# A conditioning product moved from the first expert stage's norms to behind the fourth feed-forward, with another order of work at the norm after the second cross attention

## What is computed

```python
# first block, second layer's end (x: 256 x 1024)
#   x = layer_norm(ALPHA * x + memory_cross_attention(x, mem, wq, wkv, wo), g, b)
#   x = layer_norm(ALPHA * x + ..., ...)   with swiglu_ffn: (silu(g) * u) @ w_out
# second block
for layer in range(DEPTH):                    # DEPTH = 2
    mod_l = split(silu(c)     @ ada_w[layer] + ada_b[layer], 6)
    mod_c = split(silu(c_ctx) @ ada_w[layer] + ada_b[layer], 6)
    h_l = rms_norm(lat, norm1_w[layer]) * (1.0 + mod_l[1]) + mod_l[0]
    h_c = rms_norm(cx,  norm1_w[layer]) * (1.0 + mod_c[1]) + mod_c[0]
    y_l, y_c = hyena_mixer(...) if layer == 0 else swa_mixer(...)
    lat = lat + mod_l[2] * y_l
    h_l = rms_norm(lat, norm2_w[layer]) * (1.0 + mod_l[4]) + mod_l[3]
    lat = lat + mod_l[5] * expert_choice_ffn(h_l, router[layer], w_gate[layer], w_up[layer], w_down[layer])
    # the same for cx in layer 0
return rms_norm(lat, final_norm_w)
```

## Time and profile before

| | us |
|---|---|
| median of 3 runs | 2714.54 |
| lowest, highest | 2710.27, 2716.71 |
| span of the profiled execution | 2712.6 |
| PE busy, share of the span | 2477.5, 91% |
| DVE busy | 1459.2, 54% |
| ACT busy | 503.5, 19% |
| POOL busy | 124.4, 5% |
| DMA moved | 712.30 MB, mean 263 GB/s |

### The profile page before, as it was taken

How to read it: one execution, slowest core, us unless ns; L and a number is a source line. 1 busy time by engine, 2 the same in 40 slices (tenths; PEclk the granted TensorE clock), 3 DMA queues, 4 the chain that set the end, 5 groups by cost and what they waited for, 6 DMA issues and landing times. The chain is left out here.

```text
span 2712.6 us, 37104 instructions
## 1 busy us (share of the span) xinstructions
PE 2477.5 (91%) x14598; PEld 1707.6 (63%) x14598; DVE 1459.2 (54%) x2343; ACT 503.5 (19%) x945; POOL 124.4 (5%) x134
## 2 busy tenths in 40 slices
PE   8999999999999979999999799999998987777786
PEld 8997768999999668997676333333334773333233
DVE  7768536776876558767888722232234552112113
ACT  0004414100100231003331111111110541111111
POOL 1000000000000001003221100000000000000000
PEclk9999999999999999999999999999999998888989
DMA  7668542656456456552224899999996329999997
GB/s 239 245 224 293 184 163 81 207 186 201 164 186 217 151 201 228 186 188 78 62 62 163 310 421 422 422 422 422 422 422 270 125 95 409 422 422 422 422 422 322
DMA packets 234434, 712.30 MB, mean 263 GB/s; under 512 B 12677, under 2 KB 134549, under 8 KB 178912
## 3 DMA queue, kind: packets, MB, share of 16 engines
q1 hardware_dynamic: 223328, 675.85, 64.8%
q0 software_dynamic: 9856, 32.16, 3.6%
q10 hardware_dynamic: 1152, 2.93, 0.3%
HBM read 708.69 MB, written 2.20 MB: 262 GB/s over the span
## 5 line engine op out<-in xcount | busy, mean ns | idle before, releaser
L863 PE MATMUL work<-ring,scratch 128*64 128x512 f32 (+1 forms) x3008 | 552.4, 636 | 112.7 <-DMA ring<-in_moe_up 74.2
L863 PE MATMUL work<-rows_h_parts,ring_parts 128*128 128x256 f32 x3072 | 549.7, 285 | 11.2 <-ACT rows_h_parts L1769 6.6
L863 PEld LDWEIGHTS work<-rows_h_parts,ring_parts 128*128 128x128 f32 x3072 | 477.0, 194 | 14.9 <-issue 9.8
L863 PEld LDWEIGHTS work<-ring,scratch 128*64 128x64 f32 (+1 forms) x3008 | 144.6, 126 | 496.2 <-issue 278.7
L863 PE MATMUL work<-cols_x_parts,ring_parts 128*128 128x256 f32 x1536 | 414.9, 286 | 0.0
L2207 DVE TENSOR_TENSOR ring_parts<-ring,ring_parts 128x2048 fp32r<-128x2048 f32 x132 | 302.6, 2292 | 4.5
L863 PEld LDWEIGHTS work<-cols_x_parts,ring_parts 128*128 128x128 f32 x1536 | 287.8, 195 | 1.5
L863 PE MATMUL acc<-ring_parts,rows_h_parts 128*128 128x512 f32 x960 | 279.8, 391 | 0.0
L2822 DVE COPY scratch<-work 128x512 f32<-128x512 f32 x32 | 22.1, 692 | 373.4 <-PE work L863 373.4
L863 PE MATMUL work<-scratch 128*128 128x256 f32 (+4 forms) x1040 | 197.2, 377 | 6.5 <-issue 4.2
L863 PEld LDWEIGHTS acc<-ring_parts,rows_h_parts 128*128 128x128 f32 x960 | 177.0, 188 | 35.8 <-issue 1.0
(11 more groups left out here) (314 smaller groups left out, 2893.2 us busy)
## 6 DMA issues: line engine op xcount, KB each, us to landing
ring<-in_moe_down SPq DMA_DIRECT2D x128, 1024.0 KB, 25.9
ring<-in_moe_up SPq DMA_DIRECT2D x127, 1024.0 KB, 26.6
ring<-in_moe_gate SPq DMA_DIRECT2D x121, 1024.0 KB, 25.4
ring<-in_ffn_w_in SPq DMA_DIRECT2D x88, 1024.0 KB, 7.5
ring<-in_ada_w SPq DMA_DIRECT2D x48, 1024.0 KB, 9.7
ring<-in_ffn_w_out SPq DMA_DIRECT2D x44, 1024.0 KB, 6.8
ring<-in_xa_wkv SPq DMA_DIRECT2D x16, 1024.0 KB, 6.9
ring<-in_da_w_qkv SPq DMA_DIRECT2D x12, 1024.0 KB, 7.0
```

The costliest lines, as they stand in the source:

```text
L863: ins = nc.tensor.matmul(o, lhsT, rhs, start=start, stop=stop, **kw)
```

## The change

The product `ada(3)`, with its 8 loads on SP, its copy on ACT and its `store_mods(3)` on POOL, goes from the middle of `moe_norm0` to right behind `ffn(3)`. At `xa_norm1` three orders change: PE makes `xa_out1` half by half (both token tiles' first 512 columns, then the second), with DVE's waits in `layer_norm` numbered to match; ACT copies all of the context's tiles before the two roots of `xa_norm1`, and does both roots before `ada_out(2)`; DVE splits `ffn(3)`'s first weights behind the norm (in `ffn`) instead of ahead of it. `xa_out0`, `da_out` and `sw_out` keep their order. In the cut diff the loop body that only moves by one indentation is left out.

```diff
--- before.py
+++ after.py
@@ -297,7 +297,7 @@
     norm("ctx_norm")
     norm("xa_norm1", before=[ada(2)])
     ffn(3)
-    norm("ffn_norm3", cols=False)
+    norm("ffn_norm3", before=[ada(3)], cols=False)
     norm("mod_norm0")
     chunks = D // HC
 
@@ -340,8 +340,6 @@
     plan.add("hy_out1", acc=1)
     plan.add("moe_norm0", rows=2 * NT, norms=2 * NT)
     for j in range(2 * NT):
-        if j == NT + 1:
-            ada(3)()
         plan.add(f"moe_norm0_t{j}", tiles=2)
     plan_moe(plan, 0)
     plan.add("mod_norm1", rows=2 * NT, norms=2 * NT)
@@ -362,6 +360,10 @@
     plan.add("last_norm", rows=2 * NT, norms=1)
     return plan
 
+
+TILE_BY_TILE = [(j, cb) for j in range(NT) for cb in range(2)]
+HALF_BY_HALF = [(j, cb) for cb in range(2) for j in range(NT)]
+OUT_ORDER = {"da_out": TILE_BY_TILE, "xa_out0": TILE_BY_TILE, "xa_out1": HALF_BY_HALF, "sw_out": TILE_BY_TILE}
 
 MOE_LOADS = 12
 EARLY = (3, 5)
@@ -802,6 +804,7 @@
             load_cross_attention(1)
             load_ada(2)
             ffn(3)
+            load_ada(3)
             def hand_over(n):
 
                 sp.wait_ge(loads_used, n + 1)
@@ -818,7 +821,6 @@
                 for q in range(2, HY_SLOTS):
                     hand_over(n + q)
             load_rows_out(plan["hy_out0"].loads, io["hy_w_out"], 2)
-            load_ada(3)
             def expert(layer, e, n, more, skip=0):
                 for q in range(skip, MOE_LOADS):
                     load(n, (2, D), quarter(layer, e, q), more)
@@ -1002,30 +1004,29 @@
 
                 at = plan[stage]
                 xs = (x_high, x_low)
-                for j in range(NT):
-                    if at.acc:
+                for j, cb in OUT_ORDER[stage]:
+                    if at.acc and cb == 0:
                         pe.wait_ge(acc_read, NT * at.acc - NT + j + 1)
                     c = slice(j * P, (j + 1) * P)
-                    for cb in range(2):
-                        for wp, xp in SPLIT_ORDER:
...
+                    for wp, xp in SPLIT_ORDER:
...
 
             def out_product(stage):
 
@@ -1661,6 +1662,7 @@
             ada(2)
             normed_to_cols("xa_norm1", read=False)
             ffn(3)
+            ada(3)
             for section in range(2):
                 hyena_context_first(section)
 
@@ -1677,7 +1679,6 @@
 
                         normed_to_cols("moe_norm0", h_main, read=False)
             normed_to_cols("moe_norm0", rows_h, tiles=[NT], read=False)
-            ada(3)
             normed_to_cols("moe_norm0", rows_h, tiles=[NT + 1])
             for piece in range(2):
                 read_out(pe, col_tile("moe_norm0", NT, piece))
@@ -2027,11 +2028,11 @@
             cross_attention(1)
             for j in range(NT):
                 norm_root("ctx_norm", j, NT + j)
-            cols_from_rows(col_tile("ctx_norm", 0, 0), NT * P)
-            norm_root("xa_norm1", 0, 0)
-            cols_from_rows(col_tile("ctx_norm", 1, 0), (NT + 1) * P)
+            for j in range(NT):
+                cols_from_rows(col_tile("ctx_norm", j, 0), (NT + j) * P)
+            for j in range(NT):
+                norm_root("xa_norm1", j, j)
             ada_out(2)
-            norm_root("xa_norm1", 1, 1)
             for j in range(NT):
                 split_cols("xa_norm1", j)
 
@@ -2045,6 +2046,7 @@
             for j in range(NT):
                 act.wait_ge(rows_ready, plan["ffn_norm3"].rows + j + 1)
                 act.dma_start(x_rows[j * P:(j + 1) * P, :], rows_x[:, j, :]).then_inc(x_spilled, 16)
+            ada_out(3)
 
             def hyena_high(c, section, a):
 
@@ -2144,7 +2146,6 @@
             norm_root("moe_norm0", NT, NT)
             cols_from_rows(col_tile("moe_norm0", NT, 0), NT * P)
             norm_root("moe_norm0", NT + 1, NT + 1)
-            ada_out(3)
             cols_from_rows(col_tile("moe_norm0", NT + 1, 0), (NT + 1) * P)
             experts(0)
 
@@ -2312,7 +2313,7 @@
                         half = rows_x[:, j, h * 512:(h + 1) * 512]
                         if prepare is None:
 
-                            dve.wait_ge(acc_full, 2 * (NT * use + j) + h + 1)
+                            dve.wait_ge(acc_full, 2 * NT * use + OUT_ORDER.get(acc_stage, TILE_BY_TILE).index((j, h)) + 1)
                             ins = nc.vector.scalar_tensor_tensor(out=half, in0=half, scalar=x_scale, in1=acc[:, 2 * j + h, :],
                                                                  op0=ALU.mult, op1=ALU.add)
                             if h:
@@ -2534,7 +2535,8 @@
                 if i == 1:
                     dve.wait_ge(ctx_landed, 16)
                     mod_norm("ctx_norm", [1], dst=lambda i: rows_h[:, i - NT, :])
-                split_first(2 * i + 1, 1)
+                if i == 0:
+                    split_first(1, 1)
                 layer_norm(f"xa_norm{i}", f"xa_out{i}", ALPHA, LN_EPS)
 
             def wrapped_angle(a, turns):
@@ -3169,6 +3171,7 @@
             rows_until(before_ctx + 5)
             store_mods(2)
             rows_until(before_ctx + 10)
+            store_mods(3)
             rows_until(before_ctx + 12)
             pool.wait_ge(rows_ready, plan["mod_norm0"].rows + NT)
 
@@ -3196,7 +3199,6 @@
             pool.wait_ge(mods_stored, 64 * (5 * D // SLOT + 1))
             pool.wait_ge(rows_ready, plan["moe_norm0"].rows + 1)
             load_out_gate(0, [0, 1])
-            store_mods(3)
             rows_until(before_ctx + 28)
             store_mods(4)
             store_mods(5)
```

More of the change, by code:

```diff
@@ new lines, in out_product_split @@
+                    for wp, xp in SPLIT_ORDER:
+                        if cb == 0 and xp:
+                            for piece in range(2):
+                                read_out(pe, plan[x_stage].tiles + 2 * j + piece)
+                        elif cb == 0 and not wp:
+                            high_done(x_stage, j)
+                        for half in range(2):
+                            n = at.loads + 2 * (2 * cb + half)
+                            if wp:
+                                split_done(stage, 2 * cb + half)
+                            else:
+                                weight_high_done(n)
+                            ws = parts(n, 4)
+                            for k in range(4):
+                                kk = 4 * half + k
+                                fin = bool(wp and kk == KB - 1)
+                                mm(acc[:, 2 * j + cb, :], xs[xp][:, kk, c], ws[wp][:, k, :],
+                                   kk == 0 and not wp and not xp, fin, acc_full if fin else None,
+                                   done=2 * int(bool(wp and j == NT - 1 and k == 3)))
```

18 lines of the change are left out of this document (removed).

## The result

The changed kernel takes 2696.28 us (median of 4 runs, 2695.38 to 2697.26); the kernel before, on the same chip, 2715.60 (4 runs). The ratio is 0.9931, 95% interval 0.9917 to 0.9945. The profiled execution has a span of 2693.6 us against 2712.6. Forecast was 2694.1, worked out from a kernel before of 2714.54.

The account below looks back on a forecast made before the run. The prediction took the experts as bound by DMA weight loads, with stalls at xa_norm1 second. -15 + 2 - 7.4 = -20.4 on a span of 2712.6 gave 2692.2, plus 1.9 for the median 2694.1; range 2689 to 2699, chance 0.60.

Parts of the forecast that it names:

- Part 1: At xa_norm1: the new orders remove one stall across DVE, ACT and PE; -15 us, between -12 and -16.6.
- 1.5 us set aside for a low clock: At the feed-forward's second weight half: first matmuls at 1021 run at half speed in half of the cases; 1.5 us.
- Rival (a): At xa_norm1: feed-forward's first weights stay the last thing, start moves only about 11 us; 2699.5; chance 0.13.
- Part 2: Behind ffn(3): ada(3) added on PE, partly absorbed by the wait for the norm; +2 us, bounds 0 and +8.2.
- (c): Behind ffn(3): the moved product costs its whole 8.2 us and POOL's delay adds 3; 2703.3; chance 0.08.
- (d): Behind ffn(3): the mixer waits for its weights behind eight loads, +24 us or more; 2718; chance 0.03.
- Part 3: moe_norm0 and first expert stage: without ada(3) the load queue is emptier; -7.4 us, between -4 and -9.5.
- rival (b): Expert stage gives nothing because the queue refills before 1568; -13 us, 2701.5; chance 0.10.
- PE's, set at 0 (-2 to +1): In moe_norm0: at most 1.9 us gained on PE, against possibly slow transposes and logits; 0, between -2 and +1.
- as long as before: Sign of being wrong: the stage from first expert to the end of ada(4) is not some 7 us shorter.

Follow-up runs that it names:

- tile_order: The changed kernel with PE's banks of the cross attention's output (`xa_out1`) back in the old order, tile by tile; 2694.45 us, ratio 0.9930.
- both sets in the changed kernel: The changed kernel plus idle matmuls: five between the expert norm's last two tiles, six ahead of the wait for the routing codes; 2689.45 us, ratio 0.9911.
- act_high: The changed kernel with ACT making the high parts of the feed-forward's first two weights between the roots of xa_norm1, DVE only the low parts; 2692.54 us, ratio 0.9916.
- best: The changed kernel with ACT making the high parts of the feed-forward's first two weights, and idle matmuls in PE's waits at both routings; 2687.55 us, ratio 0.9902.
- ada3_only: The kernel before with only the product `ada(3)`, its loads, copies and stores moved behind `ffn(3)`, orders at xa_norm1 old; 2710.80 us, ratio 0.9991.
- codes_before: The kernel before with only six idle matmuls added ahead of the wait for the routing codes; 2715.27 us against 2714.80, ratio 0.9999.
- split_ahead: The changed kernel with DVE's split of the feed-forward's first weights ahead of the norm again; 2702.02 us, ratio 0.9951.
- act_old: The changed kernel with ACT's old order of copies and roots at xa_norm1; 2697.22 us, ratio 0.9934.

## Why the prediction was right, and where it was not

**Part 1** (-15, measured -15.6). The path was as worked out: norm at 995.60 (3.3 us ahead of PE's last bank's end, as predicted), root behind the copies, `ada(2)` beside the norm, the split behind it, the last low parts, the second split. From the context's transposes to PE's second weight half it took 21.6 us; 20.9 was worked out. The difference is the first cast, 2.04 us instead of 1.23. The 1.5 us set aside for a low clock didn't come: the matmuls of the second half ran at 0.12 us each. The first half's 16 products were slow (3.46 us), but PE would have waited for the second split anyway, and still did, 0.44 us. Rival (a) did not come: the first load was there at 1003.4, 6.8 us ahead of its split. One reason given was wrong: the banks' new order is not what lets the norm start or the load be in time, as `tile_order` shows; both hold in the old order too.

**Part 2** (+2, measured +2.2 to the mixer's first product, +1.0 to its filters). `ada(3)` followed the feed-forward at once, the wait for the norm tile was eaten, the transposes had no gap and the first product ran at full clock (1.18 instead of 2.05 us). Another 1.2 us of slow products came back behind it. The sum had 3.4 to the first product and 1.4 back; the term that was off is `ada(3)` itself, put at 8.2 us from the earlier trace rows, where it began behind a wait (granted clock 0.66 from 1535 to 1540): right behind the feed-forward it took 7.0 (1204.66 to 1211.66). Loads, stores and POOL's low parts (1224.64) were hidden. Rivals (c) and (d) did not come.

**Part 3** (-7.4, measured -4.0). The mechanism held: the first gate loads of expert 1 took 4.8 us instead of 12.2, the chain turned to DMA at 1730.88, two experts later relative to the first (rival (b), no gain in the stage, did not come), and with PE at full clock the stage behind the first expert's start is 6.4 us shorter. The term that failed is PE's, set at 0 (-2 to +1). The rows that I had named, slow transposes after a wait of 3.89 us, were the right ones, but I followed them only to the logits and not into the first expert: up to its start PE lost only 0.7 us (1.1 gained to the logits, 1.8 lost behind them), still inside the range, but the first expert took 2.8 longer, and the stage behind its start was about 3 us longer than at full clock. The load stream was not yet full there (0.55 at 1550 to 1560), so a late PE still delayed it. Together -6.4 + 0.7 + 3.0 - 1.4 = -4.1, the -4.0 of the table but for rounding. The last term, 1.4 us less of DVE's wait for the rows in the mixer, also comes from the move and was not foreseen. The stage from the first expert was forecast 7 us shorter and was 3.3: that claim failed, though not so far as "as long as before".

**The sum** (-20.4). -15.6 + 1.0 - 4.0 = -18.6. The span fell by 19.0, the medians by 19.3. The forecast was 2.2 us too low: 1.1 because the kernel before came out at 2715.60 with its fourth run, 1.1 in the change. Part 3, 3.4 us short and at the end of its range (-4), was in part made up by part 1 (0.6), by part 2 (1.0) and by scatter (0.4). That the sum came so close is in part luck.

## What to carry to other kernels

Work that is taken out of a wait may have been holding TensorE's clock: look at the durations behind the wait, not only at the wait, and follow them until the clock is back. If nothing useful fits, a few idle matmuls into a bank that is overwritten anyway keep the level; in this case they paid only where PE, and not a full load queue, set the end (6.8 us here for both sets in the changed kernel; the second set alone brought nothing measurable in the kernel before). And undo each of several edits alone: of the three orders here, two brought all, and the third, which looked needed, nothing beside them.

## What the runs showed of the hardware

- **DVE beside POOL.** In every one of the thirteen profiles a DVE instruction that runs beside POOL's `ada_sum` addition (1.25 to 1.44 us) at `xa_norm1` ends late; only the one-column COPY or RECIPROCAL just ahead of it does not. In six it is the first cast, with 2.03 to 2.05 us instead of 1.23; in `act_high` and `best` the first subtraction, with 3.17 and 3.18 instead of 2.27; in the other five (before, `ada3_only`, `codes_before`, `split_ahead`, `act_old`) a one-column product of the norm, with 1.03 to 1.10 instead of 0.22. In `act_old`, where POOL adds from 1009.74 to 1011.00:

```profile
1009.91 1.10 DVE L2236 SCALAR_TENSOR_TENSOR rstd<-root,spread 128x1 f32<-128x1 f32 x1
```

  The Trainium skill (GPSIMD Engine Reference, "1. Specifications") lists the SBUF interface as shared with VectorE. The trace agrees, at 0.8 to 0.9 us for each time; I did not move POOL's instruction alone to see it.
- **The clock of the first expert.** Its products took 13.95, 15.3 to 15.4, or 16.7 to 16.8 us in kernels that do the same in the 30 us ahead of it (those with idle matmuls there apart). Whether the code upstream or the execution decides is open, so a gain or loss of 3 us there can't be ascribed to the edit that shifts it. A window at the lower level (1.2 GHz) reads 0.50 and one at the upper (2.4 GHz) 1.00; both profiles of the changed kernel fell the same way.
- **A full load queue can hide PE's clock:** in the profile `codes_before` gained 1.0 us ahead of the stage and lost 0.9 in it, and its median is that of the kernel before within about 2.4 us.
